# Splitting the layer inputs: rounded high part with the shift on ScalarE, low part on VectorE, GpSimd left out

## What is computed

```python
mod = silu(c) @ ada_w[L] + ada_b[L]          # three parts: shift, scale, gate
h = rmsnorm(x, norm_g[L]) * (1 + scale) + shift
x = x + gate * mixer_L(h)
# second stack
u = rmsnorm(x, norm_w[l]); x = x + mixers(u @ w_in[l]) @ w_out[l]
```

## Time and profile before

| | |
|---|---|
| median of three runs | 3158.78 us (3154.4 to 3168.04) |
| the profiled execution | 3156.09 us |
| its span, first to last instruction | 3154.4 us |
| TensorE busy | 2823.6 us, 90% |
| VectorE busy | 1607.2 us, 51% |
| GpSimd busy | 1035.0 us, 33% |
| ScalarE busy | 768.0 us, 24% |
| granted clock of TensorE, mean | 0.877 of full |

### The profile page before, as it was taken

How to read it: one execution, slowest core, us unless ns; L and a number is a source line. 1 busy time by engine, 2 the same in 40 slices (tenths; PEclk the granted TensorE clock), 3 DMA queues, 4 the chain that set the end, 5 groups by cost and what they waited for, 6 DMA issues and landing times.

```text
span 3154.4 us, 30125 instructions
## 1 busy us (share of the span) xinstructions
PE 2823.6 (90%) x11689; PEld 1953.6 (62%) x11689; DVE 1607.2 (51%) x2362; ACT 768.0 (24%) x1556; POOL 1035.0 (33%) x1008
## 2 busy tenths in 40 slices
PE   5698998998999999989988898999799898989788
PEld 4465686676988344666467574658377684648456
DVE  6855583343234455554544434764635354757442
ACT  2231211212001233133221214231322212331231
POOL 3955794367801233672310004030302005030210
PEclk8889996678778799988889897999799997999889
DMA  6330462023543000232012120213022120112111
GB/s 210 115 92 17 117 147 54 1 61 102 141 87 67 1 1 1 81 100 80 1 54 67 41 68 14 67 40 94 14 67 67 54 68 27 54 41 92 42 33 61
DMA packets 229153, 200.21 MB, mean 63 GB/s; under 512 B 86835, under 2 KB 213139, under 8 KB 228755
## 3 DMA queue, kind: packets, MB, share of 16 engines
q1 hardware_dynamic: 217491, 156.33, 17.9%
q0 software_dynamic: 11520, 41.95, 4.6%
HBM read 196.16 MB, written 2.10 MB: 63 GB/s over the span
## 4 chain that ended last, share of the span: by engine, by line
PE 71%; DVE 12%; POOL 9%; ACT 4%; issue 2%; SPq 1%; DMA 0%; DVEq 0%; ACTq 0%; POOLq 0%
PE bank L489 14%; PE bank L490 13%; PE bank L491 13%; PE bank L590 9%; PE bank L625 7%; POOL mix L2006 3%; PE bank L605 3%; PE bank L543 2%; DVE wring_parts L1357 2%; POOL mix L2003 2%; PE bank L593 1%; PE bank L753 1%; DVE whi_parts L1356 1%; PE bank L549 1%; PE bank L776 1%
## 5 line engine op out<-in xcount | busy, mean ns | idle before, releaser
L490 PE MATMUL bank<-h_parts,whi_parts 128*128 128x512 f32 (+2 forms) x1336 | 542.1, 406 | 0.0
L2032 POOL TENSOR_SCALAR pr<-pr,stat 128x256 f32<-128x256 f32 (+3 forms) x144 | 140.1, 974 | 710.0 <-DVE stat L1424 709.6
L1357 DVE TENSOR_TENSOR wring_parts<-wring,whi_parts 128x2048 fp32r<-128x2048 f32 (+1 forms) x138 | 339.9, 2463 | 4.7
L1417 DVE TENSOR_REDUCE stat<-bank 128x1 f32<-128x128 f32 (+5 forms) x320 | 149.9, 470 | 355.9 <-PE bank L593 255.6
L1356 DVE CAST whi_parts<-wring 128x2048 fp32r<-128x2048 f32 (+1 forms) x138 | 189.2, 1371 | 243.6 <-PE bank L491 205.3
L490 PEld LDWEIGHTS bank<-h_parts,whi_parts 128*128 128x128 f32 (+2 forms) x1336 | 255.3, 191 | 71.2 <-issue 7.5
L590 PE MATMUL bank<-kb,qb 64*128 64x256 f32 (+7 forms) x640 | 292.7, 543 | 7.3 <-ACT pr L1095 6.5
L625 PE MATMUL bank<-pt,vt 128*64 128x512 f32 (+3 forms) x704 | 263.6, 528 | 32.4 <-DVE pt L1438 17.7
L1095 ACT ACTIVATE pr<-bank,stat 128x128 f32<-128x128 f32 (+5 forms) x288 | 143.5, 498 | 520.5 <-DVE stat L1417 520.1
L625 PEld LDWEIGHTS bank<-pt,vt 128*64 128x64 f32 (+1 forms) x704 | 130.6, 197 | 186.1 <-issue 125.6
L489 PE MATMUL bank<-vt_parts,whi_parts 128*128 128x512 f32 (+2 forms) x472 | 199.5, 423 | 35.0 <-ACT rs L1071 12.4
(11 more groups left out here) (345 smaller groups left out, 5403.6 us busy)
## 6 DMA issues: line engine op xcount, KB each, us to landing
wring<-in_w_in SPq DMA_DIRECT2D x60, 1024.0 KB, 5.2
mix<-in_ada_w POOLq DMA_DIRECT2D x80, 512.0 KB, 4.8
wring<-in_w_out SPq DMA_DIRECT2D x16, 1024.0 KB, 5.2
wring<-in_mla_w_in SPq DMA_DIRECT2D x10, 1024.0 KB, 7.1
wring<-in_mla_w_out SPq DMA_DIRECT2D x8, 1024.0 KB, 5.4
wring<-in_swa_w_in SPq DMA_DIRECT2D x32, 256.0 KB, 4.7
wring<-in_nsa_w_in SPq DMA_DIRECT2D x32, 256.0 KB, 4.6
wring<-in_nsa_w_in SPq DMA_DIRECT2D x6, 1024.0 KB, 6.1
```

The lines of the kernel that those rows point to most:

```text
L490: pe.matmul(bank, lh, rl, start=False, stop=False)
L1357: dve.tensor_tensor(low, whole, high.bitcast(F32), ALU.subtract).then_inc(done, 1)
L1417: got = dve.tensor_reduce(top, A.tile(name)[:, 0:n], AX.X, ALU.max, negate=True)
L2032: got = pool.tensor_scalar(p_, p_, r, None, ALU.mult)
```

## The change

In layers 0 to 3 ScalarE no longer shifts h in place. It writes the high part directly from the scaled chunk, with the shift as the bias of that one instruction. VectorE makes the low part itself: (h + shift) - high in one instruction, written over h; in layers 4 and 5, where there is no shift, h - high. It does so two chunks behind its own scaling. GpSimd's low_parts is gone, and with it the semaphore h_shifted.

```diff
             def keep_high(L, k):
-                act.wait_ge(*cnt(h_shifted if L < 4 else h_scaled))
-                act.activation(h_high(L)[k], h[:, k, :], ACT.Copy).then_inc(h_kept, 1)
+                act.wait_ge(*cnt(h_scaled))
+                if L < 4:
+                    act.activation(h_high(L)[k], h[:, k, :], ACT.Identity, bias=mod[:, L, k:k + 1]).then_inc(h_kept, 1)
+                else:
+                    act.activation(h_high(L)[k], h[:, k, :], ACT.Copy).then_inc(h_kept, 1)
...
                 for k in range(KC):
-                    act.wait_ge(*cnt(h_scaled))
-                    act.activation(h[:, k, :], h[:, k, :], ACT.Identity, bias=mod[:, L, k:k + 1]).then_inc(h_shifted, 1)
-                    if k:
-                        keep_high(L, k - 1)
-                keep_high(L, KC - 1)
+                    keep_high(L, k)
...
+            def low_part(L, k):
+
+                high = h_high(L)[k].bitcast(F32)
+                dve.wait_ge(*cnt(h_scaled))
+                dve.wait_ge(*cnt(h_kept))
+                if L < 4:
+                    dve.scalar_tensor_tensor(out=h_parts[:, k, :], in0=h[:, k, :], scalar=mod[:, L, k:k + 1], in1=high,
+                                             op0=ALU.add, op1=ALU.subtract).then_inc(h_ready, 1)
+                else:
+                    dve.tensor_tensor(h_parts[:, k, :], h[:, k, :], high, ALU.subtract).then_inc(h_ready, 1)
+
             def layer_input(L, gain):
 
                 dve.wait_ge(*cnt(rstd_ready))
-                for k in range(KC):
-                    dve.scalar_tensor_tensor(out=h[:, k, :], in0=x[:, k, :], scalar=gain(k), in1=rs[:, :],
-                                             op0=ALU.mult, op1=ALU.mult).then_inc(h_scaled, 1)
+                for k in range(KC + 2):
+                    if k < KC:
+                        dve.scalar_tensor_tensor(out=h[:, k, :], in0=x[:, k, :], scalar=gain(k), in1=rs[:, :],
+                                                 op0=ALU.mult, op1=ALU.mult).then_inc(h_scaled, 1)
+                    if k >= 2:
+                        low_part(L, k - 2)
...
-            def low_parts(L):
-
-                for k in range(KC):
-                    pool.wait_ge(*cnt(h_kept))
-                    pool.tensor_tensor(h_parts[:, k, :], h[:, k, :], h_high(L)[k].bitcast(F32), ALU.subtract).then_inc(h_ready, 1)
-
             for L in STACK_1:
-                low_parts(L)
                 modulation(3 * L + 2)
...
-                low_parts(L)
                 pool.wait_ge(*cnt(decay_exp, RET_H))
```

More of the change, by code:

```diff
@@ L267, in program @@
         small_normed, lat_split = sem("small_normed"), sem("lat_split")
-        w_split, mix_split, h_shifted, h_kept, out_half = sem("w_split"), sem("mix_split"), sem("h_shifted"), sem("h_kept"), sem("out_half")
+        w_split, mix_split, h_kept, out_half = sem("w_split"), sem("mix_split"), sem("h_kept"), sem("out_half")
         max_ready, sum_ready, rinv_ready, pool_step, p_ready = sem("max_ready"), sem("sum_ready"), sem("rinv_ready"), sem("pool_step"), sem("p_ready")
```

## The result

The changed kernel takes 3190.85 us (median of four runs, 3183.71 to 3195.61), the kernel before 3157.65 in the runs beside them: ratio 1.0099, 95% interval 1.0072 to 1.0126. It is slower by 33 us; 3183 was predicted, slower, in a range from 3155 to 3203. The profiled execution took 3193.5 us, its span is 3191.8, 37.4 more than the span of before.

The account below looks back on a forecast made before the run. TensorE bounds the kernel, with 71% of the chain; other engines matter only where it stands still. Layers 0 to 5: 18.5 + 0 + 6 + 5 - 2.8 - 0.6 = +26.1 us on 3156.1, giving 3182.2; forecast 3183, range 3155 to 3203.

Parts of the forecast that it names:

- (a): GpSimd's modulation loop begins near 349 in layer 1 with no idle time before, near 38 in layer 0.
- (b): Scalings and low parts mean 1.3 to 1.6 us in layers 0 to 3, 0.75 in layers 4 and 5.
- (c): Layer 0's first matmul comes near 73 instead of 58.9, and its first block ends near 92.
- (d): TensorE's wait of 8.0 us for the modulation in layer 1 is gone.
- (e): TensorE resumes in layer 4 2.8 us sooner, counted from the layer's first scaling.
- The undisturbed gain: Start of layers 0 to 3: first scaling to TensorE's start takes 2.8 us instead of 4.67, 1.9 less a layer.
- The disturbed block: First block of layers 0 to 3: VectorE's sixteen instructions beside GpSimd's loop cost +8 us a layer, bounds 5.7 and 12.
- the factor 2.08: Slowdown of VectorE beside GpSimd's loop, from the angle table's 16.13 against 7.76 us; puts sixteen instructions at 22.3 us.
- A: Rival for layers 0 to 3: the loop does no harm, instructions stay under 1.04 us; -17, 3139 us; chance 0.1.
- B: Rival: half the harm, the loop slowed too or late in layer 0; about the same, 3170 us; chance 0.24.
- C: Worse case: upper bound 34 in layer 0, half-way to it in layers 1 to 3; +48, 3204; chance 0.1.
- D: Rival at the layer's start: TensorE's first matmul still waits for a GpSimd instruction; 3159 us; chance 0.01.

Follow-up runs that it names:

- experiment 1: Changed kernel, but in layers 0 to 3 GpSimd waits for the layer's last low part before its modulation loop: 3146.14 us, ratio to before 0.9959.
- experiment 2: Changed kernel, but GpSimd waits for the last low part in layer 0 alone, before its first two loads and loop: 3173.1 us, ratio 1.0041.

## Why the prediction was right, and where its terms were off

Times from the two profiled executions, in the order of the prediction's steps.

*Steps (a) to (e).* (a) Right: the loop of layer 0 starts at 40.51 (38 forecast), and that of layer 1 runs through its input. (b) Right in kind and just above the stated 1.3 to 1.6: low parts and scalings of layers 0 to 3 take 1.6 to 1.7 us each (25.8 to 27.5 for sixteen) where 1.39 was taken for the sum, those of layers 4 and 5 0.68 and 0.74. (c) The first matmul of layer 0 comes at 74.46 (73 forecast) and its block ends at 96.6 (92). (d) Right: in layer 1 the wait for the modulation fell from 8.0 to 0.5; TensorE's waits between 350 and 540 after the change show it beside what took its place (total, times, longest):

```profile
PE bank L489 <- DVE h_parts L1364: 15.0, 5, 9.5
...
PE bank L569 <- POOL mix L2022: 0.5, 1, 0.5
```

(e) Counted from layer 4's first scaling TensorE resumes after 24.9 us instead of 28.2, so 3.3 sooner (2.8 forecast).

*The undisturbed gain.* 1.9 a layer was forecast. In experiment 1 TensorE starts after 2.89 instead of 4.67, so 1.8 sooner, and the blocks end 1.9 to 2.5 sooner; in layer 2 nothing of that is left at the layer's end.

*The disturbed block, the term that was too small.* +8 was taken, bounds 5.7 and 12. It measured +11.0, +9.4, +10.6 and +10.6 in layers 0 to 3. The step that failed is the choice of the factor 2.08, taken from a table of angles in which five of the fourteen instructions have two inputs in SBUF. Locked out whole, which I had put beside it, would be 23.4 for sixteen; even that was short, because I let a fifth VectorE instruction pass in the pause of every turn. Four pass in eleven turns of twelve. The rows of layer 1 suggest why: behind the low part that ends at 386.47 the next instruction needs 0.74, and the loop's product starts at 387.17, 0.04 too early. One turn later the pause was 0.43 longer, and the fifth did pass. No experiment set the pause, so the reading rests on these two turns. The bound of 1.7 each, from the scalings of layer 4 before, was the truth, 27.2 against 25.8 to 27.5.

*Layer 0.* The chain ahead of the input was +14 and came as +13.1: 2.5 for the loads, 6.5 for the weighted rows (9.1 forecast), 4.1 for splits and scale (3 forecast). Then +11.0 in the block. Given back were 7.6 and not 3.5: besides the split's wait one for ScalarE's copy, behind a disturbed rotation at 188.68, went as well, since the loop was over by then. It stood in the kernel before as

```profile
PE bank L549 <- ACT raw L1039: 2.9, 1, 2.9
```

In all +16.4 (18.5 forecast); by medians experiment 2 gives 17.8, by its trace 12.2. That the sum for this layer came near is partly luck: the block was 3.0 worse than forecast and 4.1 more was given back.

*Layers 1 to 3.* Layer 1: +0.4 (0 forecast), 9.4 lost and 9.0 given back. Layer 3: +6.4 (5), but that is known only roughly: five traces with the changed kernel's instructions in layer 3 have 282.3 to 286.4 us for it, two of the kernel before 279.5 and 275.6. Layer 2 is firm, 634.8 to 638.3 in the same five against 622.2 and 622.3: **+13.6 (6), the worst miss.** Of that 2.6 is the block. The 2.0 that I had counted as given back are still there, because that wait was never the loop's. In the kernel before it ends at 876.66, and the loop was over at 867.4:

```profile
PE bank L789 <- DVE rs L1635: 2.0, 1, 2.0
```

It reads 2.0 in the kernel of experiment 1 as well. The remaining 3.0 arise between the block's end and layer 3. TensorE's idle time there has grown by 1.4 (26.5 to 27.8); the other 1.6 are matmuls that take longer in sum. Two places show it, with no idle time of TensorE in them: 37 that fill 974.2 to 984.2 before fill 1001.9 to 1013.4 after, 1.5 more, the granted clock 0.69 where it was 0.79, and 62 that fill 1003.5 to 1013.5 before fill 1032.1 to 1043.7 after, 1.6 more, 0.85 where it was 1.00; another place gives 1.3 back. The prediction had nothing for the clock outside the block. What lowered it is open; in the kernel of experiment 1, too, layer 2 keeps nothing of its 2.4 (622.2 us from scaling to scaling, 622.2 before).

*Layers 4 and 5.* Layer 4 gave 2.9 (2.8 forecast): 1.6 in the block, of which up to 1.3 may be spread (the block takes 16.3 in the second trace of before), and TensorE's wait for the copy behind the sine, 10.61 in the earlier trace rows, is shorter:

```profile
1706.48 3.78 PE L549 MATMUL bank<-raw,swap 128*128 128x512 f32 x4 [8.90 <-ACT raw L1039]
```

Layer 5's block gave 0.3 of 0.6, and 3.8 were lost in its attention by the clock, of which the prediction had nothing.

*The sum.* 13.1 + 3.3 + 0.4 + 13.6 + 6.4 - 2.9 + 3.5 = 37.4 against the forecast 26.1; by medians 33. The mechanism and the sign were right, the sum a fifth (medians) to a third (traces) too small. Some 5 of the missing 11 are matmuls at a lower clock outside the blocks, which no term of the prediction held: 1.6 in layer 2 and 3.8 in layer 5. Of the rivals, A (the loop does no harm) had its point of decision at 1.04 us an instruction, and 1.6 was measured. B lost because the loop did start early and half of the harm was not spared. C, 3204, had +34 in layer 0 where +16.4 came, and +17 in layers 1 to 3, where +20.4 came. D is out: TensorE's waits name VectorE's low parts.

## What to carry to other kernels

Before work is taken off an engine, ask what that work held back. Here eight subtractions on GpSimd were also a gate that kept a long, uncritical loop out of the start of every layer; one constant wait in their place turned the same edit from +1% to -0.4%. Before such a gain is put down to the edit, compare two traces of the same kernel layer by layer: here a layer of 280 us moved by 4 us between them. Beside GpSimd instructions that read SBUF, count one VectorE instruction with two SBUF inputs for each GpSimd instruction, one more only where GpSimd's pause is plainly longer than that instruction (0.30 + 0.93 us was not enough for a fifth, 0.73 + 0.93 was), rather than take a mean factor from another stretch. And when a helper engine's loop is waited for, move whole turns of it into that engine's idle time: that was worth more (1%) than the edit it started from.

## What had not been expected of the hardware

The exactness of the step between the two engines: 6.83 us a turn with four instructions of VectorE, and 4.45 us a pair beside the added work. That memsets on GpSimd, back to back for 37.8 us, cost VectorE nothing at all (10.2 us and 16.50, as without them). And that the granted clock of one stretch can differ between kernels whose instructions there are the same, 0.91 against 0.71 in 25 us of layer 5, worth 3.5 us, and 0.64 against 0.94 in layer 3, worth 9.6.
